# Delta rule of a four-branch mixer: block-diagonal 128x128 products stored and multiplied as 64x64 blocks in the corners of TensorE's array

## The chip, the cores and the metric

One core of one Trainium2 chip runs one program. The metric is the device time of an execution in microseconds, median of several runs. TensorE multiplies, VectorE (DVE) and ScalarE (ACT) move and combine, GpSimd (POOL) rounds weights in other stages, and SyncE (SP) issues the loads.

## The reference, cut to what matters

Three blocks follow each other on 512 tokens of width 1024. The second block's mixer has four branches; the one that matters here is `rwkv7_mix`, a delta rule with 8 heads of 64 channels:

```python
def step(s, inp):
    r_t, w_t, k_t, v_t, kk_t, a_t = inp
    sa = jnp.einsum('bhvk,bhk->bhv', s, -kk_t)
    s = (s * w_t[:, :, None, :] + sa[..., None] * (kk_t * a_t)[:, :, None, :]
         + v_t[..., None] * k_t[:, :, None, :])
    return s, jnp.einsum('bhvk,bhk->bhv', s, r_t)
...
_, y = lax.scan(step, s0, tuple(time_major(z) for z in (r, decay, k, v, kk, a)))
y = head_group_norm(y, gn_g, gn_b, RWKV_GN_EPS) + jnp.sum(r * k * r_k, axis=-1, keepdims=True) * v
return y * g
```

## The kernel before, in words

The kernel is one program of some thirty stages. Channels lie on partitions and the 512 tokens in the free dimension. Large weight products are done three times over with a high and a low part (helper line L363, rounded formats); they pass a ring of weight slices: SP loads a slice into one of two raw slots, an engine rounds it (`round`, L325), another takes the rest (`rest`, L331), which frees the raw slot for the next load, and TensorE's last matmul of the slice frees the rounded slot (`used`).

The function `rwkv` (L1070) does the delta rule in plain float32. It runs four rounds; a round takes two heads, head 0 on partitions 0 to 63 and head 1 on 64 to 127. The 512 tokens are 8 chunks of 64, and a 128-token tile `t` (four of them) holds two chunks. A matrix between the tokens of a tile is a 128x128 block of which only the two 64x64 blocks on the diagonal are used; masks such as `strict_chunk` set the rest to zero. `mt`, `nt`, `rb`, `rk`, `tri`, `inv`, `part` and `level` each hold such blocks as [128, 2 heads, 4 tiles, 128].

The order of the work is written out by hand: each engine has a program of its own for a round, and semaphores with names (`ev`) join them. On TensorE a round is:

- projections of the gate (`beside`, two slices) and of the next round's inputs (`ahead`, three slices), with the decay, lora and norm products between them, until VectorE is done with "hats" (L1377);
- `pair` (L1146): eight 64-row products for the triangle `mt` of both heads, each head on its own half of the rows; then 16 transposes (L1155), the bonus product (L1157), and 8 transposes (L1161) of the first inverse after VectorE has masked it (L1382 to L1384, `inv0`, and the copy L1390);
- the inverse in five steps, doubling the block size at each: per head four products `level` x `tri` (L1179), copied out by ACT (L1301), four of `inv` x `part` (L1198, not in the last step) and four of `part` x `inv` (L1200), subtracted by VectorE (L1415, L1416). Two chains, one per head, run in turns. Between them lie the six `side` products (L1146 again, masked by L1400), the `nv` products (L1187), and in steps 1 to 4 halves of the second and third `ahead` slice;
- `ta` and `tnv` (L1209), scaled by ACT (L1310, L1311); the growth matrices (L1214 adds the identity, L1215); the chunk updates `h` (L1219, L1220); `r` (L1224);
- the growth loop over chunks, in which state n+1 needs state n: TensorE (L1229), VectorE (L1436), with the late products (L1233, L1235) in between;
- the products with the state (L1243), gathered by VectorE and ACT (L1442, L1316), and two norm products (L1248, L1250).

VectorE's and ACT's programs have the ring's `rest` and `round` and ACT's `move` of finished `ahead` slices (L413) at fixed places between these steps:

```python
making, fetch = {1: (1, 0), 2: (1, 1), 3: (2, 0), 4: (2, 1)}, {0: 0, 2: 1}
```

Key: step, then slice and its half that TensorE makes there; `fetch` is the step after whose copies ACT moves a slice out.

Of the kernel before, what the change touches and what calls it, by code (L numbers as in the profile page):

```python
# [15 lines left out]
ALU = mybir.AluOpType  # L16
# [17 lines left out]
def tables():  # L34
# [9 lines left out]
        "strict_chunk": (s < t) & same,  # L44
# [9 lines left out]
    out["rot"] = rot  # L54
    for n in range(LEVELS):
        half = 1 << n
        block = (s // (2 * half)) == (t // (2 * half))
        out[f"level{n}"] = block & (s % (2 * half) < half) & (t % (2 * half) >= half)
# [1011 lines left out]
def rwkv(c, st, b, block, x, w_d, up_d, y, lora, keep, kept, spare, gate_d, part_out, pad, following):  # L1070
# [13 lines left out]
    state = st.sb("state", [P, NC, P])  # L1084
    landed, achain, chain, pre, stowed, zeroed = (st.sem(n) for n in ("landed", "achain", "chain", "pre", "stowed", "zeroed"))
    steps = LEVELS - 1
    ev = Events(st, lora_up=1, gates=1, kshifted=1, squared=1, normed=1, decays=1, exps=1, clamped=1, rooted=1, hats=1,
                mt_made=2, turned=1, tcopied=1, bonus_made=1, bonused=1, inv0=2, tri_made=2, side_made=6, sided=6,
                part0=steps, part1=steps, lpart0=steps, lpart1=steps, tp0=steps, tp1=steps, level0=steps, level1=steps,
                updated0=steps + 1, updated1=steps + 1, nv_made=1, nv_here=1, ta_made=1, ta_here=1, g_made=1, gt_here=1,  # L1090
                h_made=1, r_made=1, rfolded=1, grown=NC - 2, state=NC - 1, mixed=1, gathered0=1, gathered1=1, meaned=1,
                centred=1, csquared=1, varied=1, croot=1, scaled=1, affine=1, stored=1)
# [12 lines left out]
    making, fetch = {1: (1, 0), 2: (1, 1), 3: (2, 0), 4: (2, 1)}, {0: 0, 2: 1}  # L1105
# [6 lines left out]
    def growth(n):  # L1112

        return mt[:, n // TT, n % TT, :], nt[:, n // TT, n % TT, :]
# [9 lines left out]
    def _(pe):  # L1124
        def body(p, first, last_round):
            if first:
                ring.products(pe, beside[p, 0], b[1][:, :], x, DT, range(DT))
                pe.wait_ge(landed, 16)
                pe.wait_ge(pre, 3)
            for n, out in enumerate((0, 3, 6)):  # L1130
                last = pe.matmul(b[out][:, :], up[:, p, n, :], lora[:, 1 if n < 2 else 2, :], start=True, stop=True)
            ev.done(last, "lora_up")
            if not first:
                ring.products(pe, beside[p, 0], b[1][:, :], x, DT, range(DT))
# [3 lines left out]
            ev.done(pe.matmul(b[4][:, :], c.tab("head_ones"), tmp[:, :], start=True, stop=True), "normed")  # L1138
            if not last_round:
                ahead.tensor(pe, p + 1, 0, some=range(5, DT))  # L1140
            ring.products(pe, beside[p, 1], b[2][:, :], x, DT, range(DT))
# [7 lines left out]
            for h in range(2):  # L1149
                ev.done(pair(3 * h, bhat, ahat, h), "mt_made")  # L1150
            for out, src in ((4, rkv[:, 2, :]), (5, ahat[:, :]), (1, bhat[:, :]), (2, khat[:, :])):
                if out in (1, 2):
                    pe.wait_ge(gate_left, 2 * p + out)
# [3 lines left out]
            ev.done(pe.matmul(b[6][:, :], c.tab("head_ones"), tmp[:, :], start=True, stop=True), "bonus_made")  # L1157
            for h in range(2):
                ev.wait(pe, "inv0", p, h)
                for t in range(TT):  # L1160
                    last = pe.transpose(b[3 * h][:, tile_cols(t)], inv[:, h, t, :], c.tab("ident"))  # L1161
                ev.done(last, "tri_made")

            sides = [(khat, ahat, 0), (khat, ahat, 1), (bhat, rhat, 0), (bhat, rhat, 1), (khat, rhat, 0), (khat, rhat, 1)]

            def side(k):

                if k == 0:
                    ev.wait(pe, "bonused", p)
                else:  # L1170
                    ev.wait(pe, "sided", p, k - 1)
                ev.done(pair(6, *sides[k]), "side_made")

            for i in range(steps):
                for h in range(2):
                    ev.wait(pe, f"level{h}", p, i)
                    ev.wait(pe, f"updated{h}", p, i)
                    for t in range(TT):
                        last = pe.matmul(b[3 * h][:, tile_cols(t)], level[:, h, t, :], tri[:, h, t, :], start=True, stop=True)  # L1179
                    ev.done(last, f"part{h}")  # L1180
                if i < 3:
                    side(2 * i)
                if i == 3:
                    ev.wait(pe, "sided", p)
                    for h in range(2):
                        for t in range(TT):
                            last = pe.matmul(bank(6)[:, t, heads[h]], nt[:, h, t, :], v[:, t, heads[h]], start=True, stop=True)  # L1187
                    ev.done(last, "nv_made")
# [3 lines left out]
                if i == 0:  # L1192
                    ev.wait(pe, "tcopied", p)
                for h in range(2):
                    ev.wait(pe, f"lpart{h}", p, i)
                    if i < steps - 1:
                        for t in range(TT):
                            pe.matmul(b[3 * h + 1][:, tile_cols(t)], inv[:, h, t, :], part[:, h, t, :], start=True, stop=True)  # L1198
                    for t in range(TT):
                        last = pe.matmul(b[3 * h + 2][:, tile_cols(t)], part[:, h, t, :], inv[:, h, t, :], start=True, stop=True)  # L1200
                    ev.done(last, f"tp{h}")
                if i < 3:
                    side(2 * i + 1)
            ev.wait(pe, "nv_here", p)
            for h in range(2):
                ev.wait(pe, f"updated{h}", p)
                for out, r_ in ((0, ta), (3, tnv)):
                    for t in range(TT):
                        last = pe.matmul(bank(out)[:, t, heads[h]], inv[:, h, t, :], r_[:, t, heads[h]], start=True, stop=True)  # L1209
# [6 lines left out]
            ev.done(last, "g_made")  # L1216
            for n in range(NC - 1):
                out = bank(4 + n // TT)[:, n % TT, :]
                pe.matmul(out, kt[:, n % 2, n // 2, :], v[:, n // 2, :], start=True, stop=False)  # L1219
                last = pe.matmul(out, bt[:, n % 2, n // 2, :], tnv[:, n // 2, :], start=False, stop=True)  # L1220
            ev.done(last, "h_made")
            for h in range(2):
                for t in range(TT):
                    last = pe.matmul(bank(3 * h)[:, t, :], ta[:, t, :], rb[:, h, t, :], start=True, stop=True)  # L1224
            ev.done(last, "r_made")
            ev.wait(pe, "gt_here", p)
            for n in range(1, NC - 1):
                ev.wait(pe, "state", p, n - 1)
                ev.done(pe.matmul(bank(6)[:, n % TT, :], growth(n)[0], state[:, n, :], start=True, stop=True), "grown")  # L1229
                if n <= TT:  # L1230
                    t = n - 1
                    for h in range(2):
                        pe.matmul(bank(1 + h)[:, t, :], tnv[:, t, :], rb[:, h, t, :], start=t == 0, stop=False,  # L1233
                                  skip_group_check=True)
                        pe.matmul(bank(1 + h)[:, t, :], v[:, t, :], rk[:, h, t, :], start=False, stop=False,  # L1235
                                  skip_group_check=True)
            ev.wait(pe, "rfolded", p)
            for n in range(1, NC):
                cols = slice(n * CHUNK, (n + 1) * CHUNK)
                if n == NC - 1:  # L1240
                    ev.wait(pe, "state", p)
                for h in range(2):
                    last = pe.matmul(b[1 + h][:, cols], state[:, n, :], rhat[:, cols], start=False, stop=n == NC - 1,  # L1243
                                     skip_group_check=True)
# [3 lines left out]
            ev.done(pe.matmul(b[4][:, :], c.tab("head_ones"), kn[:, :], start=True, stop=True), "meaned")  # L1248
            ev.wait(pe, "csquared", p)
            ev.done(pe.matmul(b[5][:, :], c.tab("head_ones"), tmp[:, :], start=True, stop=True), "varied")  # L1250
# [3 lines left out]
    def _(act):  # L1254
# [4 lines left out]
        act.wait_ge(zeroed, 1)  # L1259
# [2584 lines left out]
```

## Time and profile before

| | before |
|---|---|
| median of 3 runs | 3968.62 us (3967.27 to 3974.47) |
| profiled execution | 3969.19 us |
| its span, first to last instruction | 3967.3 us |
| mean granted clock of TensorE | 0.983 |
| TensorE matmuls | 18060, busy 3795.7 us |
| VectorE, ScalarE, GpSimd busy | 1849.5, 1341.5, 1036.4 us |

The profile records one execution. Its time is 1.9 us above its span. A matmul's end is modelled, so the distance from one start to the next says more of its price than its duration. A plain float32 product stands as two matmuls and two weight loads (PEld).

### The profile page before, as it was taken

The numbers are of one execution on the slowest core, as the hardware profiler recorded it, in microseconds if no ns is written. First come the engines' busy times: TensorE is split into PE (matmuls) and PEld (weight loads), VectorE is DVE, ScalarE is ACT, GpSimd is POOL, SyncE is SP. The second block draws the span as 40 slices with busy tenths as digits, with TensorE's granted clock in tenths as the row PEclk, the third lists the DMA queues.
The fourth block names the chain that finished last, engine by engine and source line by source line (L and its number), as shares of the span: only waits on it lengthen the run. The fifth ranks groups of instructions, "written<-read, shape, count | busy, mean of one in ns | idle before, by whom it ended". The sixth has DMA issues, their size and how long they took to land. (4 is left out here: it accounts for less than half of the span.)

```text
span 3967.3 us, 44735 instructions
## 1 busy us (share of the span) xinstructions
PE 3795.7 (96%) x18060; PEld 3113.0 (78%) x18060; DVE 1849.5 (47%) x2793; ACT 1341.5 (34%) x2165; POOL 1036.4 (26%) x540
## 2 busy tenths in 40 slices
PE   9999989999999989999899998999999999999998
PEld 7887778887788858878777777888788888787886
DVE  3334653334533355555434545774324363333663
ACT  2223553332322243322333333433333333344332
POOL 0000235551000000001435554554344444431000
PEclk9999999999999999999989999999999999999999
DMA  4232112222222320000212223233332233211232
GB/s 151 96 96 80 48 44 74 80 80 80 85 96 95 97 82 27 27 27 18 69 53 70 80 80 98 97 99 96 100 94 86 93 99 98 70 54 53 96 96 85
DMA packets 90077, 312.42 MB, mean 79 GB/s; under 512 B 10384, under 2 KB 11152, under 8 KB 89616
## 3 DMA queue, kind: packets, MB, share of 16 engines
q1 hardware_dynamic: 89872, 309.56, 24.6%
q8 instruction: 144, 2.36, 0.2%
q14 instruction: 61, 0.50, 0.0%
HBM read 305.29 MB, written 4.19 MB: 78 GB/s over the span
## 5 line engine op out<-in xcount | busy, mean ns | idle before, releaser
L331 POOL TENSOR_TENSOR w_lo<-w_raw,w_hi 128x1024 fp32r<-128x1024 f32 (+1 forms) x353 | 854.6, 2422 | 567.3 <-ACT w_hi L325 546.1
L363 PE MATMUL s_acc<-xn_hi,w_hi 128*128 128x512 f32 x1824 | 717.4, 393 | 36.6 <-DVE xn_lo L1778 16.1
L363 PE MATMUL s_acc<-xn_lo,w_hi 128*128 128x512 f32 x1824 | 712.8, 391 | 0.0
L363 PE MATMUL s_acc<-xn_hi,w_lo 128*128 128x512 f32 x1824 | 712.2, 390 | 0.0
L325 ACT ACTIVATE w_hi<-w_raw 128x1024 fp32r<-128x1024 f32 (+2 forms) x421 | 434.0, 1032 | 602.8 <-PE s_acc L363 501.5
L350 POOL CAST w_hi<-w_raw 128x1024 fp32r<-128x1024 f32 (+1 forms) x167 | 176.3, 1056 | 1595.5 <-DVE w_lo L331 877.8
L331 DVE TENSOR_TENSOR w_lo<-w_raw,w_hi 128x1024 fp32r<-128x1024 f32 (+1 forms) x235 | 283.2, 1205 | 362.4 <-ACT w_hi L325 361.6
L363 PEld LDWEIGHTS s_acc<-xn_hi,w_hi 128*128 128x128 f32 x1824 | 344.2, 189 | 113.6 <-DVE xn_lo L1778 17.7
L363 PEld LDWEIGHTS s_acc<-xn_lo,w_hi 128*128 128x128 f32 x1824 | 344.6, 189 | 72.0 <-issue 1.2
L363 PEld LDWEIGHTS s_acc<-xn_hi,w_lo 128*128 128x128 f32 x1824 | 344.2, 189 | 72.1
L363 PE MATMUL s_acc<-hidden_hi,w_hi 128*128 128x512 f32 x784 | 305.0, 389 | 0.0
L363 PE MATMUL s_acc<-hidden_lo,w_hi 128*128 128x512 f32 x784 | 305.0, 389 | 0.0
L363 PE MATMUL s_acc<-hidden_hi,w_lo 128*128 128x512 f32 x784 | 305.0, 389 | 0.0
L363 PE MATMUL rw_b<-xn_hi,w_hi 128*128 128x512 f32 x600 | 250.8, 418 | 2.8 <-DVE part L2399 1.8
L363 PE MATMUL rw_b<-xn_lo,w_hi 128*128 128x512 f32 x600 | 237.0, 395 | 0.0
L363 PE MATMUL rw_b<-xn_hi,w_lo 128*128 128x512 f32 x600 | 236.8, 395 | 0.0
L363 PEld LDWEIGHTS s_acc<-hidden_lo,w_hi 128*128 128x128 f32 x784 | 147.1, 188 | 30.6
L363 PEld LDWEIGHTS s_acc<-hidden_hi,w_hi 128*128 128x128 f32 x784 | 147.1, 188 | 30.5
L363 PEld LDWEIGHTS s_acc<-hidden_hi,w_lo 128*128 128x128 f32 x784 | 147.1, 188 | 30.5
L1813 DVE TENSOR_TENSOR x<-x,s_acc 128x512 f32<-128x512 f32 x48 | 33.0, 687 | 278.8 <-PE s_acc L363 278.8
L363 PE MATMUL hg_b<-xn_hi,w_hi 128*128 128x512 f32 x352 | 143.3, 407 | 12.8 <-ACT gates_h L2386 5.2
L363 PEld LDWEIGHTS rw_b<-xn_hi,w_hi 128*128 128x128 f32 x600 | 115.1, 192 | 32.5 <-issue 6.7
(640 smaller groups left out, 6458.5 us busy)
## 6 DMA issues: line engine op xcount, KB each, us to landing
w_raw<-in_f_up SPq DMA_DIRECT2D x132, 512.0 KB, 3.7
w_raw<-in_mg_w SPq DMA_DIRECT2D x64, 512.0 KB, 3.6
w_raw<-in_g_up SPq DMA_DIRECT2D x64, 512.0 KB, 3.6
w_raw<-in_f_down SPq DMA_DIRECT2D x48, 512.0 KB, 3.5
w_raw<-in_hg_w SPq DMA_DIRECT2D x32, 512.0 KB, 3.9
w_raw<-in_g_down SPq DMA_DIRECT2D x32, 512.0 KB, 3.7
w_raw<-in_fox_w SPq DMA_DIRECT2D x24, 512.0 KB, 3.6
w_raw<-in_f_down SPq DMA_DIRECT2D x24, 384.0 KB, 3.1
```

The costliest lines, as they stand in the source:

```text
L325: act.activation(hi, raw, ACT.Copy).then_inc(self.rounded, 1)
L331: eng.tensor_tensor(lo, raw, value, ALU.subtract).then_inc(self.parted, 1)
L350: pool.tensor_copy(hi, raw).then_inc(self.rounded, 1)
L363: last = pe.matmul(out, w[:, slot, tile_cols(k)], v[:, k0 + k, :], start=start and k == 0 and n == 0, stop=stop and k == kt - 1 and n == 2)
L1813: made = dve.tensor_tensor(x[:, t, :], x[:, t, :], self.acc(t), ALU.add)
```

## The change

All matrices between tokens are stored as their 64x64 blocks alone, [128, 2 heads, 4 tiles, 64], chunk 0 of a tile on partitions 0 to 63 and chunk 1 on 64 to 127. Every product of them is made per chunk and head, with 64 rows and 64 columns of the array; consecutive products lie in different corners, and the PSUM banks are assigned so that consecutive ones write different banks. The two chains of the inverse are no longer the two heads but the two halves of the tokens (`k`), each with both heads; `level` has two buffers. The transposed triangle is computed (`ahat` x `bhat`) instead of transposed. `tri`, `inv`, `level` and `part` operations on VectorE and ACT have 128x256 elements. The transposes of `bhat` and `khat` move into steps 0 and 1. `tnv` is scaled by VectorE. The identity in the growth matrices is added by VectorE. The second half of the third `ahead` slice moves from step 4 to the growth loop, the first half from step 3 to step 4. The tables have 64 columns for the masks.

The diff, cut to its core:

```diff
-    bt, kt = st.sb("bt", [P, 2, TT, P]), st.sb("kt", [P, 2, TT, P])
-    v, ta, tnv = (st.sb(n, [P, TT, P]) for n in ("v", "ta", "tnv"))
-    mt, nt, rb, rk = (st.sb(n, [P, 2, TT, P]) for n in ("mt", "nt", "rb", "rk"))
-    tri, inv, part, level = spare
+    v, ta, tnv, bt, kt = (st.sb(n, [P, TT, P]) for n in ("v", "ta", "tnv", "bt", "kt"))
+    mt, nt, rb, rk = (st.sb(n, [P, 2, TT, CHUNK]) for n in ("mt", "nt", "rb", "rk"))
+    tri, inv, part, level = *spare[:3], spare[3:]
+    gt, ht, state = st.sb("gt", [P, NC - 2, P]), st.sb("ht", [P, NC, CHUNK]), st.sb("state", [P, NC, CHUNK])
...
-    making, fetch = {1: (1, 0), 2: (1, 1), 3: (2, 0), 4: (2, 1)}, {0: 0, 2: 1}
+    making, fetch = {1: (1, 0), 2: (1, 1), 4: (2, 0)}, {0: 0, 2: 1}
+    def inner(k, n):
+        return banks[:, 2 * k:2 * k + 2, n * P:(n + 1) * P].rearrange("p h (t f) -> p h t f", t=2)
+    def of(k, tile):
+        return tile[:, :, 2 * k:2 * k + 2, :]
...
-            def pair(out, l, r_, h):
-                for t in range(TT):
-                    last = pe.matmul(b[out][:, tile_cols(t)], l[heads[h], tile_cols(t)], r_[heads[h], tile_cols(t)],
-                                     start=True, stop=True)
+            def pair(out, t, l, r_):
+                for n in range(2):
+                    for h in range(2):
+                        cols = chunk(t, n)
+                        last = pe.matmul(out[heads[n], h, :], l[heads[h], cols], r_[heads[h], cols], start=True, stop=True)
                 return last
+            def blocks(k, n, l, r_):
+                for turn in range(2):
+                    for t in (2 * k, 2 * k + 1):
+                        for h in range(2):
+                            rows = heads[(h + turn) % 2]
+                            last = pe.matmul(inner(k, n)[rows, h, t % 2, :], l[rows, h, t, :], r_[rows, h, t, :], start=True, stop=True)
+                return last
+            for k in range(2):
+                if k == 1:
+                    pe.wait_ge(gate_left, 2 * p + 2)
+                for t in range(2):
+                    pair(inner(k, 0)[:, :, t, :], 2 * k + t, bhat, ahat)
+                    last = pair(inner(k, 1)[:, :, t, :], 2 * k + t, ahat, bhat)
+                ev.done(last, "mt_made")
...
             for i in range(steps):
+                for k in range(2):
+                    ev.wait(pe, f"level{k}", p, i)
+                    ev.wait(pe, f"updated{k}", p, i)
+                    ev.done(blocks(k, 0, level[i % 2], tri), f"part{k}")
+                if i == 0:
+                    ev.wait(pe, "bonused", p)
+                    turn(bhat, "bturned")
...
                 if i in making and not last_round:
                     piece, half = making[i]
                     ahead.tensor(pe, p + 1, piece, some=range(half * DT // 2, (half + 1) * DT // 2))
+                for k in range(2):
+                    ev.wait(pe, f"lpart{k}", p, i)
+                    if i < steps - 1:
+                        blocks(k, 1, inv, part)
+                    ev.done(blocks(k, 2, part, inv), f"tp{k}")
+                if i < 3:
+                    side(i)
+                if i == 1:
+                    ev.wait(pe, "bcopied", p)
+                    turn(khat, "kturned")
...
             for n in range(1, NC - 1):
-                out = bank(1 + n // TT)[:, n % TT, :]
-                pe.matmul(out, c.tab("ident"), c.tab("ident"), start=True, stop=False)
-                last = pe.matmul(out, ta[:, n // 2, :], bt[:, n % 2, n // 2, :], start=False, stop=True)
+                rows, t, at = heads[n % 2], n // 2, (n - 1) // 2 * CHUNK
+                for h in range(2):
+                    last = pe.matmul(b[3 - n % 2][heads[h], at:at + CHUNK], ta[rows, t, heads[h]], bt[rows, t, heads[h]],
+                                     start=True, stop=True)
...
             for n in range(1, NC - 1):
                 ev.wait(pe, "state", p, n - 1)
-                ev.done(pe.matmul(bank(6)[:, n % TT, :], growth(n)[0], state[:, n, :], start=True, stop=True), "grown")
+                at = n % 2 * CHUNK
+                ev.done(pe.matmul(b[6][:, at:at + CHUNK], gt[:, n - 1, :], before(n), start=True, stop=True), "grown")
...
+                if 2 <= n and not last_round:
+                    if n < NC - 2:
+                        ahead.tensor(pe, p + 1, 2, some=range(DT // 2 + n - 2, DT // 2 + n - 1))
...
+            for k in range(2):
+                ev.wait(dve, "mt_made", p, k)
+                q.free(dve.tensor_tensor(of(k, mt), inner(k, 0), wide("own_strict"), ALU.mult))
+                q(dve.tensor_tensor(of(k, tri), inner(k, 1), wide("level0_turned"), ALU.mult))
+                q.free(dve.tensor_tensor(of(k, inv), of(k, mt), wide("level0"), ALU.mult))
+                ev.done(dve.tensor_tensor(of(k, level[0]), of(k, mt), wide("level1"), ALU.mult), f"level{k}")
+                q(dve.tensor_tensor(of(k, tri), wide("own_ident"), of(k, tri), ALU.subtract))
+                ev.done(dve.tensor_tensor(of(k, inv), wide("own_ident"), of(k, inv), ALU.subtract), f"updated{k}")
...
+            ev.wait(dve, "ta_made", p)
+            ev.done(dve.tensor_scalar(tnv[:, :, :], bank(1), -1.0, None, ALU.mult), "tnv_here")
```

## Rows read from the trace of the kernel before

**Rows 1.** The page: span, TensorE, and two groups of the weight ring.

```profile
span 3967.3 us, 44735 instructions
PE 3795.7 (96%) x18060; PEld 3113.0 (78%) x18060; DVE 1849.5 (47%) x2793; ACT 1341.5 (34%) x2165; POOL 1036.4 (26%) x540
...
L325 ACT ACTIVATE w_hi<-w_raw 128x1024 fp32r<-128x1024 f32 (+2 forms) x421 | 434.0, 1032 | 602.8 <-PE s_acc L363 501.5
...
L331 DVE TENSOR_TENSOR w_lo<-w_raw,w_hi 128x1024 fp32r<-128x1024 f32 (+1 forms) x235 | 283.2, 1205 | 362.4 <-ACT w_hi L325 361.6
```

**Rows 2.** Windows, TensorE alone, from "hats" to the state products, four rounds.

```profile
core 0: us, PE busy (x), PEclk, DMA share, GB/s
1485.30:1561.84 76.54, 71.65 (x550) 1.00 0.09 28
...
1793.30:1858.71 65.41, 60.62 (x502) 1.00 0.04 13
```

**Rows 3.** The same windows, matmuls of line L363 alone.

```profile
1485.30:1561.84 76.54, 12.05 (x48) 1.00 0.09 28
```

**Rows 4.** Windows, all engines, the inverse loop of round 0.

```profile
core 0: us, PE busy (x) PEld busy (x) DVE busy (x) ACT busy (x) POOL busy (x), PEclk, DMA share, GB/s
1492.80:1539.40 46.60, 45.95 (x336) 42.22 (x337) 26.02 (x37) 9.55 (x15) 0.00 (x0) 1.00 0.14 46
```

**Rows 5.** Timeline of TensorE, round 0: start, duration, line, operands, count.

```profile
1485.34 1.71 PE L1146 MATMUL rw_b<-rw_ahat,rw_bhat 64*128 64x128 f32 x16 [0.42 <-DVE rw_tmp L1377]
...
1494.83 1.16 PE L1146 MATMUL rw_b<-rw_ahat,rw_khat 64*128 64x128 f32 x8
1495.91 1.16 PE L1198 MATMUL rw_b<-rw_part,rw_inv 128*128 128x128 f32 x8
1496.91 1.06 PE L1200 MATMUL rw_b<-rw_inv,rw_part 128*128 128x128 f32 x8
1497.80 1.06 PE L1198 MATMUL rw_b<-rw_part,rw_inv 128*128 128x128 f32 x8
```

**Rows 6.** Windows, TensorE, line L1146 alone: before and around the change of head.

```profile
1485.33:1485.88 0.55, 0.54 (x4) 1.00 0.00 0
1485.88:1486.23 0.35, 0.35 (x9) 1.00 0.00 0
```

**Rows 7.** Lines L2602 and L1243: durations in ns, minimum, median, maximum, and forms.

```profile
L2602 PEld LDWEIGHTS hg_b<-hg_v,hg_kt x112: 187/192/192, 603.6 to 912.4; 128*128 128x128 f32 x112
L2602 PEld LDWEIGHTS rw_b<-gla_v,gla_kt x56: 132/137/137, 1913.5 to 2022.5; 128*64 128x64 f32 x56
L1243 PE MATMUL rw_b<-rw_rhat,rw_state x112: 222/275/275, 1558.6 to 1858.4; 128*128 128x64 f32 x112
```

**Rows 8.** Lines of TensorE, all rounds: busy us, mean ns, idle before, releaser.

```profile
L1179 PE MATMUL rw_b<-rw_tri,rw_level 128*128 128x128 f32 x320 | 41.5, 281 | 7.8 <-DVE rw_tri L1390 5.5 <-DVE rw_inv L1416 2.3
L1229 PE MATMUL rw_b<-rw_state,rw_mt 128*128 128x128 f32 x48 | 10.1, 292 | 4.4 <-DVE rw_state L1436 4.4
L1214 PE MATMUL rw_b<-table 128*128 128x128 f32 x48 | 9.7, 284 | 4.7 <-ACT rw_tnv L1311 4.7
L1161 PE MATMUL rw_b<-table,rw_inv 128*128 128x128 f32 x32 | 5.0, 280 | 2.2 <-DVE rw_inv L1384 2.2
```

**Rows 9.** Timelines of ACT and DVE, round 0.

```profile
1543.69 0.59 ACT L1311 ACTIVATE rw_tnv<-rw_b 128x512 f32<-128x512 f32 x1
...
1552.52 0.35 DVE L1436 SCALAR_TENSOR_TENSOR rw_state<-rw_b,rw_wfull,rw_nt 128x128 f32<-128x128 f32 x1 [1.47 <-PE rw_b L1229]
...
1561.84 0.68 DVE L1442 COPY rw_kn<-rw_b 64x512 f32<-64x512 f32 x1 [2.65 <-PE rw_b L1243]
```

**Rows 10.** Windows, TensorE and its granted clock, two stretches and their next; a timeline row.

```profile
1562.03:1565.44 3.41, 1.41 (x3) 1.00 0.00 0
1565.44:1568.85 3.41, 3.41 (x9) 1.00 0.51 154
2143.30:2146.70 3.40, 2.10 (x7) 1.00 0.33 108
2146.70:2150.10 3.40, 3.40 (x12) 0.50 0.12 44
...
2144.70 2.62 PE L2824 MATMUL rw_b<-ml_qk 64*128 64x512 f32 x8 [1.30 <-ACT ml_e L2863]
```

More of the change, by code:

```diff
@@ L1067, in wait, with rwkv @@
         eng.wait_ge(self.sems[name], r * self.per[name] + i + 1)
[L1070 removed]
+def rwkv(c, st, banks, b, block, x, w_d, up_d, y, lora, keep, kept, spare, gate_d, part_out, pad, following):
     st.sb("pad_held", [P, 3, S + 1])
@@ L1126, in body @@
             if first:
-                ring.products(pe, beside[p, 0], b[1][:, :], x, DT, range(DT))
+                ring.products(pe, beside[p, 0], b[2][:, :], x, DT, range(DT))
                 pe.wait_ge(landed, 16)
                 pe.wait_ge(pre, 3)
-            for n, out in enumerate((0, 3, 6)):
+            for n, out in enumerate((0, 4, 6)):
                 last = pe.matmul(b[out][:, :], up[:, p, n, :], lora[:, 1 if n < 2 else 2, :], start=True, stop=True)
@@ L1133, in body @@
             if not first:
-                ring.products(pe, beside[p, 0], b[1][:, :], x, DT, range(DT))
+                ring.products(pe, beside[p, 0], b[2][:, :], x, DT, range(DT))
             if not last_round:
@@ L1156, in body @@
             ev.done(last, "turned")
[L1157 to L1164, printed above, removed]
+            sides = [(khat, ahat), (bhat, rhat), (khat, rhat)]
@@ L1166, in side @@
             def side(k):
                 if k == 0:
-                    ev.wait(pe, "bonused", p)
+                    ev.wait(pe, "tcopied", p)
                 else:
                     ev.wait(pe, "sided", p, k - 1)
-                ev.done(pair(6, *sides[k]), "side_made")
-            for i in range(steps):
[L1175 to L1182, printed above, removed]
+                for t in range(TT):
+                    last = pair(banks[:, 4:6, t * CHUNK:(t + 1) * CHUNK], t, *sides[k])
@@ L1183, in body @@
                 if i == 3:
                     ev.wait(pe, "sided", p)
-                    for h in range(2):
+                    for swap in range(2):
                         for t in range(TT):
-                            last = pe.matmul(bank(6)[:, t, heads[h]], nt[:, h, t, :], v[:, t, heads[h]], start=True, stop=True)
+                            for h in range(2):
+                                rows = heads[(h + swap) % 2]
+                                last = pe.matmul(banks[rows, 4 + h, t * CHUNK:(t + 1) * CHUNK], nt[rows, h, t, :], v[rows, t, heads[h]],
+                                                 start=True, stop=True)
@@ L1191, in body @@
                     ahead.tensor(pe, p + 1, piece, some=range(half * DT // 2, (half + 1) * DT // 2))
-                if i == 0:
-                    ev.wait(pe, "tcopied", p)
-                for h in range(2):
[L1195 to L1209, printed above, removed]
+                for k in range(2):
[8 more added lines that the diff above has]
+                    turn(khat, "kturned")
+            ev.wait(pe, "nv_here", p)
+            for k in range(2):
+                ev.wait(pe, f"updated{k}", p)
+                for h in range(2):
+                    for swap in range(2):
+                        for t in (2 * k, 2 * k + 1):
+                            for out, r_, rows in ((0, ta, heads[swap]), (1, tnv, heads[1 - swap])):
+                                last = pe.matmul(bank(out)[rows, t, heads[h]], inv[rows, h, t, :], r_[rows, t, heads[h]],
+                                                 start=True, stop=True)
             ev.done(last, "ta_made")
@@ L1225, in body, with before @@
+            ev.done(last, "h_made")
+            for t in range(TT):
+                for h in range(2):
+                    for n in range(2):
+                        rows = heads[n]
+                        last = pe.matmul(b[n][heads[h], t * CHUNK:(t + 1) * CHUNK], ta[rows, t, heads[h]], rb[rows, h, t, :],
+                                         start=True, stop=True)
             ev.done(last, "r_made")
             ev.wait(pe, "gt_here", p)
+            def before(n):
+                return ht[:, 0, :] if n == 1 else state[:, n, :]
@@ L1291, in body @@
             ev.wait(act, "turned", p)
-            for dst, n in ((bt, 1), (kt, 2)):
-                for half in range(2):
-                    rows = heads[half]
-                    q.free(act.activation(dst[rows, half, :, :], b[n][rows, :].rearrange(by_tile, t=TT), ACT.Copy))
             q.free(act.activation(v[:, :, :], bank(4), ACT.Copy))
@@ new lines, in body @@
+            ev.done(last, "gt_here")
+            ev.wait(dve, "h_made", p)
+            ends = wfull[:, :].rearrange("p (t n f) -> p n t f", n=2, t=TT)[:, :, :, CHUNK - 1:CHUNK]
+            for m in range(2):
+                made = TT - m
+                last = dve.tensor_tensor(ht[:, :, :].rearrange("p (t n) f -> p n t f", n=2)[:, m, 0:made, :],
+                                         b[4 + m][:, 0:made * CHUNK].rearrange("p (t f) -> p t f", t=made),
+                                         ends[:, m, 0:made, :].broadcast_to([P, made, CHUNK]), ALU.mult)
+                if m == 0:
+                    ev.done(last, "state")
+                else:
+                    q(last)
```

200 lines of the change are left out of this document (102 added, 98 removed).

## The prediction

> **What bounds the kernel now.** I read the page first: TensorE is busy 3795.7 of 3967.3 us [rows 1], and its chain of work ends on TensorE too. An average over stages says little, so I looked at what the diff touches, the delta rule of `rwkv`, which runs in four rounds. From "hats" to the last mixing product a round takes 76.5 us with 550 matmuls in three rounds, 65.4 us with 502 in the last [rows 2]; of these, L363 (projections riding along) has 48, in 12.05 us, and in the last round none [rows 3]. The view by stage of round 0 has TensorE busy 45.95 of the inverse loop's 46.60 us, VectorE 26.02, ScalarE 9.55 [rows 4]. So the matmul stream sets the length of these four stretches, some 295 us together. The rest of the program is as before.
>
> How a product is paid for: every plain float32 product is two matmuls, each with its own weight load, and eight of them in a row take 0.89 us, 0.112 us each [rows 5]. It makes no difference whether 64 or 128 rows or columns are used: the 64-row products of L1146 also go at that pace.
>
> **What a product of half the width costs.** The new code replaces most 128x128 products by 64x64 ones: about twice as many instructions, each with half the weight columns and half the moving columns. Weight loads of 64 columns last 137 ns against 192, and the shortest matmul with 64 moving columns 222 against 275 [rows 7]: 64 columns are worth 55 ns on either side. One chain would so go at about 112 - 55 = 57 ns, the same total as now. The gain must come from corners working side by side. This trace has one place for it: L1146 in front of the loop, where head 0 uses rows 0 to 63 and head 1 rows 64 to 127. Sixteen matmuls there last 1.71 us in all [rows 5], and in the 0.35 us around the change of head nine are in flight, against four in the 0.55 us before it [rows 6]. Two row groups do run beside each other, each at 0.112 us, one matmul per 56 ns together. Bounds for the new pace: 56 ns, the densest that is shown, and 29 ns, two chains of 57 ns with nothing in between. I take 40 ns, near the middle: the overlap is shown and speaks for 29, but weight loads have to be issued too, and the densest stretch has no more than one instruction per 28 ns.
>
> The Trainium skill, "TensorEngine Tiling (Array Packing)", section Instruction Overhead, speaks against the change: each matmul has some 60 cycles of overhead on trn2, so nothing should be gained by tiling a dimension that is already small. 60 cycles of 2.4 GHz are 25 ns; if weight load and matmul each paid it, the estimate would be 50 ns, and by it the sum below would give 3943. No row shows an instruction that short.
>
> **The sum, per round.**
> Products. Before: 550 - 48 (L363) = 502 matmuls [rows 2, 3], of which 24 are transposes (16 at L1155, 8 at L1161) and 2 the 512-wide bonus product, so 476, x 0.112 = 53.3; the transposes at the same price 2.7. After, from the diff: 32 products for the first triangle and its turned copy, 48 for the sides, 224 in the inverse (80 + 64 + 80), 16 nv, 32 for ta and tnv, 12 growth (the 6 additions of the identity on TensorE go, DVE adds it), 28 h, 16 r, 32 late ones, 14 with the state: 454, or 908 matmuls at 40 ns = 36.3; 6 full-array growth steps, 12 x 0.112 = 1.3; 16 transposes 1.8. Gain 56.0 - 39.4 = 16.6 us; at 29 ns 26.6, at 56 ns 2.1.
>
> Switches between 64-row and full-array work. Eight products of L1146 take 1.08 us to the next line's start instead of 0.89 [rows 5]: 0.19 us each. Before, seven groups of 64-row products make 14. After: bonus and transposes 2, two turns 4, three projection halves 6, the growth loop 8, its two ends 2, 22 in all. Cost 8 x 0.19 = 1.5 us; nothing, if a narrower tile switches freely.
>
> Waits. Before, TensorE's idle times there, summed over the rounds, come to (7.8 + 2.2 + 4.7 + 4.4) / 4 = 4.8 us a round [rows 8]. A DVE operation on 128x256 I put at 0.42 us, between 0.35 for 128x128 and 0.68 for 512 columns [rows 9]; at 0.35 the masks gain 0.8 us a round, at 0.68 masks and loop lose some 6 us, 24 in all. (a) The masks: the transpose of the first inverse and its copy go; six operations a half make 2.3 us, so the first half is ready at about 3.9 us from "hats", while TensorE still has 4.5 us of products and transposes; the second at 6.2, so one wait of 1.2. (b) Inside the loop each chain's copy (ACT) and two subtractions (DVE) need about 0.8 and 1.15 us with latency; the other chain's products take 0.64 and 1.28, and sides, turns, nv and projections lie between: about 0.7 in steps 3 and 4 together. DVE has at most 4.1 us a step (two levels, four subtractions, a side, one 1.2 us rest of the ring, [rows 1]) against 5.1 of TensorE. (c) ACT loses tnv's scaling (0.59, [rows 9]), which goes to DVE and is needed only by h: 1.2 becomes about 0.95. (d) The growth loop stays at about 1.1, with state updates of 64 columns. Together 4.0: 0.8 saved; at 29 ns the cover is thinner, and I take 0.7 lost.
>
> Moved. The second half of the third projection piece goes from step 4 into growth steps 2 to 5. Its twelve matmuls cost TensorE the same and fill those waits. Behind it come ACT's move (0.6, as its other copies of 512 columns) and the rounding of the next round's second gate slice (1.03, [rows 1]), now just before the gather of the mixed rows. TensorE then still has growth step 6 and the state products, about 2.3 us against 1.6: hidden; were that cover gone, it costs at most 1.6 us in each of three rounds. SP's queue loads wait for DVE's rests, which stay in their places in the step order, so loads are only closer together, at a DMA share of 0.14 now [rows 4]; POOL has no work here. ACT's b and k copies move into steps 0 and 1, behind the copies that the chain wants and long before the h products: nothing. The gathers halve, 0.68 to 0.42: 0.3 saved.
>
> Sum: 16.6 - 1.5 + 0.8 + 0.3 = 16.2 us, x 4 = 65. At 29 ns 24.7 x 4 = 99; at 56 ns 1.7 x 4 = 7. The profiled execution took 3969.2 us, 1.9 over its span and 0.6 over the median of the three runs: 3969 - 65 = 3904.
>
> **The rivals.**
> *Full overlap.* Both row groups run at 57 ns and nothing else limits: 3870. For it: the side-by-side stretch lost nothing on either head. Against: nothing here issues that fast.
> *No overlap to speak of* (issue-bound at 28 ns an instruction, or two banks or corners that exclude each other; then the change doesn't do what it says): 3962. For it: no denser pace is in the trace. Against: [rows 6] has two chains at their full pace.
> *The granted clock falls, slower.* In one stretch with 2.10 of 3.40 us busy, its last part 64-row products (L2824), the clock stood at 1.00 and was 0.50 in the next; in another with only 1.41 of 3.41 us busy, all of it full-array, it stayed at 1.00 [rows 10]. The new loop has nothing but 64-row products between projections. At 1.2 GHz the 908 matmuls go at 56 ns at best, (908 x 0.056 and 6.2 for the wider ones, 1.0 us more than now), L363's 12 us and the bonus product's 0.9 double, the switches cost 22 x 0.38 - 14 x 0.19 = 5.7 more, the gathers give 0.3: 19 us lost in each of three rounds and 7 in the last, 4033 if it holds all through. It decides from some 45% of the stretch at half clock on, since full clock gives 16. Against: in the delta stretches the clock is 1.00 throughout now [rows 2], though L1146 is among them, and the projection halves and gates are dense.
>
> **How the numbers follow.** Chances: forecast 0.45, full overlap 0.22, no overlap 0.19, clock 0.14. The forecast's own range, from 34 to 48 ns by the same sum, is 3885 to 3934. The range 3860 to 3968 holds the first three and leaves out a clock that stays low for most of it. What a measurement of this kernel can tell from no change is 0.2%, 8 us. Faster by more: forecast, full overlap, and half of the no-overlap case (3962 lies near the edge of 3960.7): 0.77. Same: 0.09. Slower: 0.14.
>
> **What would show it.** Right: a round's delta stretch of about 60 us instead of 76.5; the inverse lines with matmuls of 64x64 form beginning 30 to 50 ns apart; granted clock 1.00 there; four subtractions a step on DVE at 0.42. TensorE's matmuls rise from 18060 to 18060 + 4 x (12 + 908 - 476 - 8) = 19804. Wrong: a pace of 55 ns or more, clock 0.50 in the loop, idle times of TensorE ended by ACT's part copies or DVE's subtractions that come to more than about 6 us a round, or projections of L363 that start late for a rest or a load.

## The result, and the profile after

The changed kernel took 3852.0 us (median of 4 runs, 3849.9 to 3854.3), the kernel before 3970.1 beside it: a ratio of 0.9699, with a 95% interval of 0.9686 to 0.9711. That is 118 us less. The forecast was 65 us less, 3904, and the result lies 8 us below the low end of its range. The sign was right, the size was not: the gain is nearly twice the forecast.

The profiled execution took 3850.4 us against 3969.2, so 118.8 less. The first lines of its page answer to [rows 1]:

```profile
span 3848.6 us, 48163 instructions
PE 3682.0 (96%) x19804; PEld 2997.7 (78%) x19804; DVE 1795.6 (47%) x2768; ACT 1326.5 (34%) x2153; POOL 1036.8 (27%) x540
```

There are 19804 matmuls, as counted ahead from the diff, 1744 more than before, and yet TensorE is busy 113.7 us less. Where that comes from stands in the windows from "hats" to the last state product. Columns as in [rows 2]; the second and fourth rows are the stretches between two rounds, the last is the whole stage:

```profile
1485.63:1532.90 47.27, 43.82 (x986) 0.96 0.15 47
1532.90:1559.19 26.29, 23.67 (x84) 0.94 0.07 21
1559.19:1604.85 45.66, 42.29 (x986) 1.00 0.16 49
1604.85:1631.03 26.18, 23.56 (x84) 0.93 0.07 20
...
1702.49:1737.02 34.53, 30.88 (x938) 1.00 0.09 26
1485.63:1737.02 251.39, 226.42 (x4124) 0.97 0.12 37
```

Against [rows 2], 76.54 has become 47.27 in round 0, and 65.41 has become 34.53 in the last: 29.3 and 30.9 less. With 30.8 each in the rounds between, the four stretches give 121.8 us where 65 were forecast, some 30 a round instead of 16.2. About 3 us are lost elsewhere: the code behind this stage, the same in both kernels, took 3848.6 - 1737.0 = 2111.6 us instead of 3967.3 - 1858.7 = 2108.6 (the end of the last window of [rows 2]). Whether that is a cost of the change is not shown. The same code took between 2110 and 2119 us in the profiles of the experiments below, and of the kernel before there is one profile, while its executions lie between 3966.6 and 3977.7 us.

Why a stretch shrank so far is seen in TensorE's timeline, round 1 (start, duration, line, operands, count):

```profile
1573.06 0.63 PE L1174 MATMUL rw_b<-rw_inv,rw_part 64*64 64x64 f32 x16
1573.52 0.63 PE L1174 MATMUL rw_b<-rw_part,rw_inv 64*64 64x64 f32 x16
...
1574.45 0.64 PE L1165 MATMUL rw_b<-rw_rhat,rw_bhat 64*64 64x64 f32 x30
```

Read the starts, not the durations. A group of 16 matmuls of the inverse (L1174; eight products), alternating over the two diagonal corners of the array, is followed by the next 0.46 us later: 0.029 us per matmul. The sides (L1165), which go round all four corners, put 30 matmuls into some 0.43 us (the last 0.22 us of the 0.64 are one matmul's own length): 0.0145 us each. The prediction took 0.040 for both.

The waits of TensorE, all rounds, answer to [rows 8]:

```profile
L1174 PE MATMUL rw_b<-rw_tri,rw_level_a 64*64 64x64 f32 x384 | 15.6, 222 | 8.1 <-DVE rw_inv L1443 7.0 <-DVE rw_inv L1466 1.0
L1252 PE MATMUL rw_b<-rw_bt,rw_ta 64*64 64x64 f32 x96 | 2.3, 226 | 2.8 <-ACT rw_ta L1367 2.8
L1278 PE MATMUL rw_b<-rw_state,rw_gt 128*128 128x64 f32 x40 | 7.4, 267 | 0.5 <-DVE rw_state L1494 0.4
L1278 PE MATMUL rw_b<-rw_ht,rw_gt 128*128 128x64 f32 x8 | 1.6, 284 | 1.5 <-DVE rw_ht L1484 1.5
```

They come to (8.1 + 2.8 + 0.5 + 1.5) / 4 = 3.2 us a round, with 0.1 more at L1245. A faster TensorE has not run into its helpers: the largest wait, 7.0 / 4 = 1.75 a round, is for the masks in front of the first step, most of it (1.57 in round 1) for those of the second token half.

### The profile page after: what moved, and what is told of

It is laid out like the page before. It is cut to its first block and busy times, and to the rows that moved or that the text cites. A ratio compares the mean times of both kernels' runs of the same rounds, so it can differ in the third digit from the quotient of the medians.

```text
span 3848.6 us, 48163 instructions
## 1 busy us (share of the span) xinstructions
PE 3682.0 (96%) x19804; PEld 2997.7 (78%) x19804; DVE 1795.6 (47%) x2768; ACT 1326.5 (34%) x2153; POOL 1036.8 (27%) x540
```

## The experiments

Theory 1, formed from these rows: each corner of the array is a chain of its own, one 64x64 matmul per 58 ns, and all four run side by side, so the pace is 58 ns by the number of corners that neighbouring instructions use. Its rivals: a pace set by issuing alone; side-by-side work only between row groups, which is all that the trace of before showed; an overlap that comes from neighbours writing different banks. And a rival about the whole: shorter waits gave the gain, not the pace.

**Runs in one corner.** The inverse keeps its instructions, but takes four products in one corner and then four in the other.

```
-                            rows = heads[(h + turn) % 2]
+                            rows = heads[turn]
```

> The inverse's half-width products come in runs of four in one corner of the array (both heads, two tiles) before the other corner gets its four, instead of changing corner with each one; same number of instructions. Theory 1 (each corner is a chain of its own at about 58 ns per 64x64 matmul, and corners overlap only where neighbouring instructions use different ones): a call of 16 matmuls, now 0.47 us, takes about 0.7 to 0.9 us; 14 calls in four steps and the first triangle's part per half, 28 calls a round: 6 to 12 us a round of which idle time of TensorE hides little, so 3875 to 3900 us. Rival (the pace of 29 ns is a limit of issuing and knows no corners): 3852, no change. Rival (queue ahead deep enough to start the second corner's instructions early): between, under +10 us.

Measured: 3867.2 us, ratio 0.9732 (0.9716 to 0.9748), so 13 to 15 us slower than the change. Its timeline in round 1:

```profile
1581.24 0.27 PE L1174 MATMUL rw_b<-rw_part,rw_inv 64*64 64x64 f32 x1
1581.30 0.22 PE L1174 MATMUL rw_b<-rw_inv,rw_part 64*64 64x64 f32 x1
1581.35 0.22 PE L1174 MATMUL rw_b<-rw_part,rw_inv 64*64 64x64 f32 x1
1581.35 0.22 PE L1174 MATMUL rw_b<-rw_inv,rw_part 64*64 64x64 f32 x1
1581.41 0.22 PE L1174 MATMUL rw_b<-rw_part,rw_inv 64*64 64x64 f32 x1
1581.41 0.22 PE L1174 MATMUL rw_b<-rw_inv,rw_part 64*64 64x64 f32 x1
1581.47 0.56 PE L1174 MATMUL rw_b<-rw_part,rw_inv 64*64 64x64 f32 x10
1581.82 0.27 PE L1174 MATMUL rw_b<-rw_inv,rw_part 64*64 64x64 f32 x1
```

Two chains are interleaved here: "part, inv" starts at 1581.35, .41, .47, "inv, part" at 1581.30, .35, .41, each 0.06 us apart. A call of 16 matmuls lasts 1581.82 - 1581.24 = 0.58 us, 0.036 us each: not 0.058, because the next corner's run begins while the last three of the eight before it are still to come. The issue rival (no change) falls, and so does theory 1's own size of 0.7 to 0.9 us a call: TensorE looks a few instructions ahead, the third reading, which put the loss too low at under 10 us. The kernel also shows what the pace is worth: 448 inverse matmuls a round x 4 rounds x 0.007 to 0.008 us is 12.5 to 14 us. That the whole loss is as large is in part luck. The profiled execution, the slowest of its four with 3871.2 us, has each stretch 5.2 to 6.4 us longer than with the change, of which the pace explains some 3.4; the stretches also have pieces at half clock (granted 0.50), as the change has in round 0 alone. Round 1:

```profile
1564.24:1615.24 51.00, 48.10 (x986) 0.97 0.14 44
```

The stage is 18 us longer in all, as the tails are 4 us shorter. The pace that the prediction took, 0.040, is close to what this order has.

**One bank for two neighbours.**

```
-                for turn in range(2):
+                for h in range(2):
                     for t in (2 * k, 2 * k + 1):
-                        for h in range(2):
+                        for turn in range(2):
```

> The inverse's products alternate over the two corners as now, but two neighbours write the two partition halves of one PSUM bank instead of two banks. Theory 1 (only the corner counts): a call stays at 0.47 us and the time at 3852, within 4 us. Rival (what lets neighbours overlap is that they write different banks): a call goes to about 0.9 us, 28 calls a round, so up to 12 us a round and 3900.

Measured: 3851.8 us, ratio 0.9693 (0.9678 to 0.9707); the stretch of round 1 takes the same 45.7 us as with the change.

```profile
1553.99:1599.68 45.69, 42.33 (x986) 1.00 0.16 49
```

The bank rival falls. The Trainium skill, "TensorEngine Tiling (Array Packing)", section Gotcha 1: PSUM Pressure, has it that different row tiles can't access one PSUM bank at the same time. Here neighbours in two row groups write the two halves of one bank, and nothing is lost.

**Which corners overlap.** Side 0 stays in one row group for sixteen matmuls and alternates its two column groups; side 1 stays in one column group and alternates the row groups; side 2 is as in the change; the first triangle goes corner by corner.

```
...
-                for t in range(TT):
-                    last = pair(banks[:, 4:6, t * CHUNK:(t + 1) * CHUNK], t, *sides[k])
+                every = [(n, h, t) for t in range(TT) for n in range(2) for h in range(2)]
+                if k == 0:
+                    every = [(n, h, t) for h in range(2) for t in range(TT) for n in range(2)]
+                if k == 1:
+                    every = [(n, h, t) for n in range(2) for t in range(TT) for h in range(2)]
```

> One look at paces. Side 0 takes one row group at a time with the two column groups in turn, side 1 one column group at a time with the two row groups in turn, side 2 goes round all four corners as now; the first triangle's products go corner by corner in runs of eight matmuls. Theory 1 (corners are independent, each at about 58 ns): 29, 29, 14.6 and 58 ns per matmul. Rival (only row groups run side by side, as the trace of the kernel before showed): side 0 at 58 and side 1 at 29. Rival (issue sets the pace): 14.6 to 29 everywhere, also in runs.

Windows of this kernel, TensorE, the sides alone (three rows: sides 0 and 1, each within its first sixteen matmuls, and side 2) and the triangle alone (the fourth):

```profile
1563.61:1563.85 0.24, 0.24 (x9) 1.00 0.79 119
1570.27:1570.51 0.24, 0.24 (x10) 1.00 0.00 0
1577.65:1577.89 0.24, 0.24 (x19) 1.00 0.33 102
1554.30:1556.50 2.20, 2.20 (x61) 1.00 0.00 0
```

9 and 10 matmuls in 0.24 us with two corners, in one row group as well as in one column group; 19 with four corners; 61 in 2.20 us, 0.036 each, in runs, the pace of the first experiment and not the 58 ns that theory 1 expected. So column groups run beside each other just as row groups do, and the rival that rested on the trace of before falls. The Trainium skill, "TensorE: Matmul & The Clock Gate", section Part 3: Packing small matmuls — row/col tiling, lists a measured speedup of 10.6 for row and column tiles together, sixteen of 32x32 with other shapes than here; that both kinds go side by side agrees with these rows. The program, 3849.4 us in its one run, is no slower than the change: in round 1 the stretch is 46.86 instead of 45.66 us, but the tail behind it kept the full clock, 24.67 instead of 26.18.

**The products of one line twice.** The third product of a step is made a second time: 160 matmuls more a round.

```
+                    blocks(k, 2, part, inv)
                     ev.done(blocks(k, 2, part, inv), f"tp{k}")
```

> The third product of each inverse step (L1174, part by inverse) is made twice, 160 matmuls more a round, 640 in all, nothing else changed. If TensorE's stream of products still sets the delta stretches at 29 ns each, less what the doubled work covers of waits: 4.7 us a round, 15 to 19 us, 3867 to 3871. If waits between the chains set them now: under 6 us. If a product still costs 40 ns, as the prediction took it: 25 us, 3877.

Measured: 3868.0 us, ratio 0.9735 (0.9722 to 0.9749): 14 to 16 us more. Round 1:

```profile
1561.39:1611.49 50.10, 46.66 (x1146) 1.00 0.15 45
```

50.10 - 45.66 = 4.44 us for 160 matmuls, 0.028 each: nearly their whole pace. So TensorE's stream still sets these stretches, at 0.029 a matmul and not at 0.040. The rival that only waits got shorter falls too: they went from 4.8 to 3.3 us a round, 1.5 of the 30.

**Both halves in step.** TensorE waits for both halves before each group of a step.

```
                 for k in range(2):
                     ev.wait(pe, f"level{k}", p, i)
                     ev.wait(pe, f"updated{k}", p, i)
+                for k in range(2):
                     ev.done(blocks(k, 0, level[i % 2], tri), f"part{k}")
```

and the same for the waits on "lpart".

> Before each of a step's two groups TensorE waits for both halves' copies or subtractions, so that the two chains by token half move in step as one. If the gain is one of pace alone: no more than 4 us. If splitting in two chains is what keeps the faster products fed: each of the two waits in five steps is late by about one DVE or ACT operation (0.42 and 0.4 us) and the other half's products (0.47 to 0.94) no longer cover: 7 to 10 us a round, 3880 to 3892.

Measured: 3858.3 us, ratio 0.9711 (0.9694 to 0.9728): 5 to 6 us more, between the two; the intervals overlap, but the stage alone grows from 251.4 to 258.2 us. Its waits and its windows of round 1, of the tail behind it and of the last round:

```profile
L1174 PE MATMUL rw_b<-rw_tri,rw_level_a 64*64 64x64 f32 x384 | 14.3, 225 | 13.5 <-DVE rw_inv L1445 9.7 <-DVE rw_inv L1468 3.8
L1174 PE MATMUL rw_b<-rw_tri,rw_level_b 64*64 64x64 f32 x256 | 9.2, 220 | 3.9 <-DVE rw_inv L1468 3.9
```

```profile
1558.89:1606.44 47.55, 41.89 (x986) 1.00 0.15 47
1606.44:1631.11 24.67, 22.06 (x84) 1.00 0.07 21
...
1704.59:1743.29 38.70, 30.94 (x938) 1.00 0.08 23
```

The waits for VectorE grow from 8.1 to 17.4 us over the four rounds, the stretches by 1.8, 1.9, 3.4 (with a piece at half clock) and 4.2 us: most in the last round, which has no projection halves. So the split in two chains is worth some 10 us of the stretches' 121.8. The expectation of 7 to 10 a round took every step's wait as uncovered, but projection halves, sides and turns cover most. The loss in time is smaller because the tails are 4.5 us shorter: two of the three kept the full clock here.

**The projection half back in step 4.**

```
-    making, fetch = {1: (1, 0), 2: (1, 1), 4: (2, 0)}, {0: 0, 2: 1}
+    making, fetch = {1: (1, 0), 2: (1, 1), 3: (2, 0), 4: (2, 1)}, {0: 0, 2: 1}
```

and no piece in the growth loop.

> The second half of the third projection piece stays in step 4 of the inverse, as before the change, and is not in the growth loop. Prediction's reading (its twelve matmuls cost the same and fill waits of the growth loop; the rounding behind it is hidden): without the fill the growth steps of rounds 0 to 2 last as long as those of the last round (0.85 us a step against 1.48), step 4 is 3 us longer, the chain of state updates shows as waits of TensorE: 1 to 2 us a round lost, +3 to +6. Rival (what moved only made the gather late: it starts 0.3 us after the last mixing product): -1 us.

Measured: 3859.6 us, ratio 0.9714 (0.9701 to 0.9727). The interval overlaps that of the change, but the stage alone is 258.7 us long instead of 251.4. The size fits the first reading, its reason explains less than half of it. Round 0, in which both kernels have the same mean clock and one piece at half clock, from "hats" to the first growth step and from there to the last state product, first with the change, then with the half moved back:

```profile
1485.63:1525.22 39.59, 36.20 (x871) 0.96 0.18 56
1525.22:1532.90 7.68, 7.63 (x116) 1.00 0.01 2
```

```profile
1481.82:1524.50 42.68, 39.30 (x882) 0.96 0.17 52
1524.50:1530.05 5.55, 5.13 (x104) 1.00 0.01 3
```

The twelve projection matmuls cost 3.1 us in front of the growth loop and 2.1 in it, so filling its waits gains 1.0 us a round, 3 of the 7.3. The rest is the clock: in rounds 1 and 2 of this kernel it falls at the end of the growth loop, and the last round, whose code is the same as with the change, has a piece at half clock too (36.0 us instead of 34.5), as it has in the second profile of the changed kernel (36.1), so this part need not come from the edit. Windows of this kernel at the end of round 1's growth loop and behind it:

```profile
1597.80:1601.20 3.40, 3.02 (x66) 1.00 0.00 0
1601.20:1604.60 3.40, 2.81 (x31) 0.50 0.02 5
```

The thinner growth steps are followed by half clock from 1601.20 on; with the change the same place stays at 1.00 until the tail. But thin growth steps are not enough for it: in round 0 here (5.55 us at 1.00), and in the last round with the change, which has none of the projection matmuls either, the clock stays.

**A further version.** The next round's three low-rank products go into the waits of a round's tail, ScalarE rounds the slice behind its gathers, and side 0 goes between the two halves of the first step.

```
             ev.done(last, "mixed")
+            if not last_round:
+                lora_up(p + 1, (0,))
...
+            if not last_round:
+                lora_up(p + 1, (1, 2))
...
```

> A further version: the next round's three low-rank products (L1147) are issued in the waits of a round's tail instead of ahead of the next front, ScalarE rounds the last slice behind the gathers instead of ahead of them, and the first side goes between the two halves of the first step, where TensorE waits for the second half's masks. Waits filled: tail 2.9 us of products a round for three rounds of which some 2 us go into waits, masks 0.5 us a round, gather 0.26 us in three rounds: -6 to -9 us, 3843 to 3846. Rival (what is taken from the waits is given back, as the front waits for loads or gates, or the clock falls elsewhere): 3852 or above.

It took 3846.8 us, ratio 0.9682 (0.9669 to 0.9696), with runs from 3836 to 3850. A second set of runs was made on one chip beside the change itself and beside a version that makes the first inverse last:

```
-                    ev.wait(pe, f"updated{k}", p, i)
+                    if i == 0:
+                        ev.wait(pe, f"tri{k}", p)
+                    else:
+                        ev.wait(pe, f"updated{k}", p, i)
...
```

> The version with the filled tail again, beside the next one on the same chip, as its first five runs spread over 14 us: the ratio to the kernel before should come to 0.967 to 0.969 again.

> The changed kernel itself on the same chip, as the common measure of the two versions: 0.969 to 0.971 of the kernel before.

> The version with the filled tail, and in the masks of the first step VectorE makes, for both halves, the mask, the turned triangle and the first level before it makes either half of the first inverse; the first products wait for the turned triangle, the second and third for the inverse. The wait of TensorE in front of the second half's first products (some 1.6 us a round with the change alone, 0.55 us with the first side in between) ends two operations of 0.38 us earlier, and the inverse is wanted only a copy later: 0.5 to 1 us a round, -2 to -4 us beside the version with the filled tail, some 3842. Rival (the wait only moves to the second and third products, which want the inverse): no change.

Measured: filled tail 3847.5, ratio 0.9692 (0.9679 to 0.9706); the change 3845.7, 0.9699 (0.9684 to 0.9714); inverse last 3844.2, 0.9684 (0.9671 to 0.9698). The intervals overlap: no version is shown to beat the change. The stage itself did become shorter, from 251.2 us with the change on that chip to 245.1 and 247.2 (windows of the whole stage: the change, the filled tail, the inverse last):

```profile
1480.59:1731.83 251.24, 226.48 (x4124) 0.97 0.12 37
```

```profile
1484.89:1730.02 245.13, 221.69 (x4124) 0.99 0.12 38
```

```profile
1482.66:1729.89 247.23, 226.28 (x4124) 0.97 0.12 37
```

but 4 to 6 us are within what the unchanged rest of the program varies by. Its tail behind round 1, 24.2 us, is only 0.5 under the 24.7 of the kernel with both halves in step, which has the old tail at full clock; so of the 2 us between 26.2 and 24.2 most is the clock. The rival "given back" is seen too: in the first runs of this version, the front's wait for ScalarE at the normalising product is 10.0 us over the rounds, where it was 3.3. And the masks' wait, halved by the moved side, shortened no stretch: the second half's first products still begin 5.56 us after "hats" (1564.75 - 1559.19 with the change), when VectorE's twelve mask operations are done. With the inverse last they begin earlier, and 0.25 us a round is left of the 0.5 to 1 expected (45.41 us in round 1), since side 0 then waits for ScalarE's copy (0.56 us in round 1).

## Why the prediction was wrong

**What bounds the kernel: right.** TensorE's stream sets the four stretches, before and after: 4.44 of 4.7 us of doubled products showed in the time.

**The pace: the step that failed.** The prediction bounded the pace by "56 ns, the densest that is shown, and 29 ns, two chains of 57 ns with nothing in between", took 40, and priced all 908 matmuls by it. Its 57 ns for one chain, worked out from the 55 ns that 64 columns save, was right: 58 was measured. There was luck in it, as L1243 of [rows 7], with only the moving operand 64 wide, still has 28 matmuls in 3.24 us, the last one's own 0.22 included: 0.112 each. Wrong was what stands side by side. The lower end was drawn from row groups, since [rows 6] shows no others, and so it was no bound: column groups overlap too. And 40, the middle, supposed a cost of issuing that isn't there, as 14.5 ns shows. Of the 908, 572 use two corners (inverse 448, nv 32, ta and tnv 64, state 28) and 336 go round four (triangle 64, sides 96, growth 24, h 56, r 32, late 64): 572 x 0.0294 + 336 x 0.0146 = 16.8 + 4.9 = 21.7 us instead of 36.3, with all 336 at the price of the sides. This term alone is 14.6 us a round, 58 in four: 6.1 a round because two corners go at the lower end of the range, 8.5 because four go below it. 65 + 58 = 123 us against the 121.8 that the stretches gained; the other terms, below, nearly cancel. The full-overlap rival, 3870, came nearest, and stopped at the same false bound.

By the rule on overhead per matmul in the Trainium skill ("TensorEngine Tiling (Array Packing)", Instruction Overhead) the sum came out at 3943 (worked out again, 50 ns gives 7.1 us a round and 3941). These rows speak against the rule as a price of the stream: a matmul with a weight load of its own goes every 14.5 ns, less than the 25 ns that the prediction read from the page for either of them. Against an overhead inside one corner they say nothing, as its 58 ns are more than twice 25.

**Switches: right where they can be read.** 22 at 0.19 us were taken. A projection half between two groups of the inverse, in TensorE's timeline of round 1, shows two of them:

```profile
1575.61 1.15 PE L1174 MATMUL rw_b<-rw_tri,rw_level_a 64*64 64x64 f32 x32
1576.69 0.50 PE L365 MATMUL rw_b<-xn_hi,w_hi 128*128 128x512 f32 x1
1577.02 0.40 PE L365 MATMUL rw_b<-xn_lo,w_hi 128*128 128x512 f32 x1
...
1579.31 0.39 PE L365 MATMUL rw_b<-xn_hi,w_lo 128*128 128x512 f32 x1
1579.63 0.68 PE L1174 MATMUL rw_b<-rw_part,rw_inv 64*64 64x64 f32 x16
1580.14 0.63 PE L1174 MATMUL rw_b<-rw_inv,rw_part 64*64 64x64 f32 x16
```

By the starts, the 32 matmuls ahead take 1.08 us instead of 0.94, the first and the last projection matmul 0.33 and 0.32 instead of 0.23, and the first group behind 0.51 instead of 0.47: 0.37 for the two. The half moved back agrees, with two changes more in front of the growth loop: 3.09 us for twelve matmuls that take 2.72 at 0.227 each.

**Waits: 4.0 forecast, 3.3 measured.** The second half's masks cost 1.75 instead of 1.2, the loop's steps 0.25 instead of 0.7, ta 0.7 instead of 0.95, the growth loop 0.5 instead of 1.1. A VectorE operation on 128x256 took 0.42, as put in.

**Moved: right on TensorE, wrong on ScalarE.** The projection pieces fill waits of the growth loop, worth 1.0 us a round. But the move and the rounding ahead of the gather were called hidden, with 2.3 us of cover against 1.6, and they are not quite, in ScalarE's timeline of round 1 and TensorE's row behind it:

```profile
1603.69 0.60 ACT L415 ACTIVATE rw_pad<-rw_b 128x512 f32<-128x512 f32 x1 [8.96 <-PE rw_b L365]
1604.18 1.05 ACT L327 ACTIVATE w_hi<-w_raw 128x1024 fp32r<-128x1024 f32 x1
1605.13 0.38 ACT L1372 ACTIVATE rw_kn<-rw_b 128x256 f32<-128x256 f32 x1
...
1605.65 0.67 PE L1303 MATMUL rw_b<-rw_kn,table 128*128 128x512 f32 x1 [0.82 <-ACT rw_kn L1372]
```

The state products, at the new pace, are done by 1604.83, and the gather starts at 1605.13. The same wait is 0.56 where the half is back in step 4, so 0.26 us in each of three rounds, and the 0.3 counted for the smaller gathers is gone. A cover that is itself made faster by the change has to be costed at the new pace.

**The clock: in small part.** The rival's 4033 didn't come; three of the four stretches stand at 1.00. But the claim of 1.00 throughout was too much: round 0 is 0.96, and each tail has a piece at half clock, as these windows of the changed kernel show, round 0's first step and the tail behind round 1:

```profile
1488.36:1491.77 3.41, 1.61 (x36) 1.00 0.00 0
1491.77:1495.18 3.41, 3.41 (x52) 0.50 0.17 30
...
1604.42:1607.83 3.41, 1.51 (x17) 1.00 0.00 0
1607.83:1611.24 3.41, 3.04 (x4) 0.50 0.45 127
```

Before these two falls TensorE was busy 1.61 and 1.51 of 3.41 us; round 1's first step, with the same wait for masks, has no fall. Round 0 is 47.27 us long where round 1, with the same work, is 45.66: 1.6 us for one such piece. The tails of 26.2 us are 24.7 where no fall comes. They are no loss against the kernel before, which had half clock there too: its three tails are 24.66, 27.63 and 26.25 us long, 78.5 together against 78.3 now.

## What to carry to other kernels

Price a product that fills only a corner of TensorE's array by its own chain (58 ns for each of the two matmuls of a 64x64 float32 product, weight load included), and divide by the number of corners that neighbouring instructions use; order the loops so that they use different ones. A pace seen in a trace bounds the new one only if what set it there still sets it in the new code: without a row that shows a limit of issuing, the price has no floor there. And whatever covers a moved step is costed at the speed it has after the change.

## What was not expected of the hardware

Two row groups of one column group, two column groups of one row group, and all four corners run side by side with no loss that shows: 9, 10 and 19 matmuls in 0.24 us. Two neighbours may write the two halves of one bank at that pace. In runs of eight in one corner the next corner begins after five, so the pace is 0.036 us and not 0.058. And work put into TensorE's waits can be worth more than the waits it fills: the projection pieces in the growth loop save 1.0 us a round, and without them the stage takes 7.3 us more, as half clock came at the end of that loop in two rounds of three. Why the clock fell in some tails and not in others with the same code was not settled; what the engine did before each is all that was seen. How much of the rest is owed to the thinner loop stays open; with the half moved back a fall came behind a stretch that is 3.02 of 3.40 us busy, with the growth loop's short matmuls alone.
